# Two token blocks read as rows and transposed on TensorE, K and Q weights stored by head, W2 at other addresses

## The reference

```python
xn = rmsnorm(x, norm_mix_g)
u = xn @ w_in                       # 5120 columns: b, c, v (512 each) | q, k, v (512 each) | 2 x 1024 gates
y_a = (b_g * causal_conv3(c_g * v_a)) @ w_a_out
o = diff_attention(q, k, v, lam, alibi_slopes)   # 4 heads, two softmax maps of width 64, values of 128
y_b = (rmsnorm(o, subln_g) * (1 - lam_init)) @ w_b_out
x = x + (sigmoid(gate_a) * y_a + sigmoid(gate_b) * y_b) @ w_o
h = rmsnorm(x, norm_mlp_g) @ w_mlp_in            # 4096 columns
x = x + square(relu(h)) @ w_mlp_out
return rmsnorm(x, norm_final_g)
```

## Time and profile before

| | |
|---|---|
| time, median of 3 runs (lowest to highest) | 1285.27 us (1283.91 to 1289.87) |
| the profiled execution, its own time | 1275.98 us |
| its span, slowest core (core 4) | 1274.5 us |
| spans of all cores | 1249.3 to 1274.5 us |
| TensorE busy, instructions | 1155.0 us (91%), 7066 |
| ScalarE, VectorE, GpSimd busy | 541.4 us (42%), 472.9 us (37%), 90.9 us (7%) |
| chain that ended last, by engine | PE 75%, DMA 8%, ACT 4%, DVE 4%, issue 4% |
| of it, by line | L404 (all matmuls) 75%, DMA of W2 4%, ACT L677 4%, DMA of xs 2%, DMA of wc 2% |
| TensorE waiting for the loads of W2 (core 4) | 28.9 us in 15 waits |

### The profile page before, as it was taken

How to read it: one execution, slowest core, us unless ns; L and a number is a source line. 1 busy time by engine, 2 the same in 40 slices (tenths; PEclk the granted TensorE clock), 3 DMA queues, 4 the chain that set the end, 5 groups by cost and what they waited for, 6 DMA issues and landing times.

```text
span 1274.5 us, 20401 instructions; the slowest of 8 cores (1249.3 to 1274.5 us)
## 1 busy us (share of the span) xinstructions
PE 1155.0 (91%) x7066; PEld 553.3 (43%) x7066; DVE 472.9 (37%) x1079; ACT 541.4 (42%) x740; POOL 90.9 (7%) x148
## 2 busy tenths in 40 slices
PE   6887788998999999999999999937999999999996
PEld 3343444444444454454444444412444444444442
DVE  2437367465345534324445534200222222122211
ACT  0385665586556787777623223300033013103300
POOL 3212101010001001000000002000000000000000
PEclk9989899998999999999999999966999999999998
DMA  9965723230216437375294708940130003012001
GB/s 155 244 180 100 149 84 72 74 79 10 38 44 128 95 63 151 53 173 135 37 233 116 231 1 184 194 112 6 67 99 1 33 33 99 2 58 75 1 34 50
DMA packets 67412, 117.75 MB, mean 92 GB/s; under 512 B 37072, under 2 KB 39376, under 8 KB 66288
## 3 DMA queue, kind: packets, MB, share of 16 engines
q0 software_dynamic: 14544, 44.11, 20.5%
q1 hardware_dynamic: 52768, 72.34, 19.4%
HBM read 120.69 MB, written 29.36 MB: 118 GB/s over the span
## 4 chain that ended last, share of the span: by engine, by line
PE 75%; DMA 8%; ACT 4%; DVE 4%; issue 4%; another core or an unknown queue 2%; POOL 1%; DVEq 0%; ACTq 0%; SPq 0%; POOLq 0%
PE ps_all L404 75%; DMA big<-w 4%; ACT big L677 4%; DMA big<-xs 2%; DMA big<-wc 2%; POOL big L409 1%; ACT big L448 1%; DVE big L624 0%; DMA xm_sp<-big 0%; DVE big L615 0%; DVE big L617 0%; DMA big<-xT 0%; DVE big L819 0%; DVE big L558 0%
## 5 line engine op out<-in xcount | busy, mean ns | idle before, releaser
L404 PE MATMUL ps_all<-big 128*128 128x512 bf16 (+7 forms) x7066 | 1155.0, 329 | 107.0 <-DMA big<-w 28.9
L404 PEld LDWEIGHTS ps_all<-big 128*128 128x128 bf16 (+2 forms) x7066 | 553.3, 99 | 708.2 <-issue 266.7
L677 ACT ACTIVATE big<-ps_all,big 128x1024 bf16<-128x1024 f32 (+3 forms) x384 | 337.6, 926 | 122.9 <-PE ps_all L404 110.0
L920 ACT ACTIVATE big<-ps_all 128x512 bf16<-128x512 f32 x128 | 76.3, 597 | 140.8 <-PE ps_all L404 140.5
L937 ACT ACTIVATE big<-big 128x1024 bf16<-128x1024 f32 x16 | 16.9, 1056 | 247.3 <-DVE big L932 247.3
L921 DVE TENSOR_TENSOR big<-big 128x512 bf16<-128x512 bf16 x128 | 54.5, 425 | 159.9 <-ACT big L920 159.5
L932 DVE SCALAR_TENSOR_TENSOR big<-ps_all,big 128x512 f32<-128x512 f32 x32 | 24.0, 751 | 199.1 <-PE ps_all L404 199.1
L819 DVE SCALAR_TENSOR_TENSOR big<-big,ps_all 128x512 f32<-128x512 f32 x64 | 43.8, 687 | 115.1 <-PE ps_all L404 114.7
L808 ACT ACTIVATE big<-ps_all,big 128x512 f32<-128x512 f32 x64 | 43.6, 686 | 81.4 <-PE ps_all L404 81.4
L448 ACT ACTIVATE big<-big 128x1024 bf16<-128x1024 f32 x32 | 33.8, 1057 | 39.1 <-DMA big<-xs 38.3
L939 POOL TENSOR_TENSOR big<-big 128x1 f32<-128x1 f32 x16 | 8.7, 545 | 461.7 <-DVE big L938 461.7
(11 more groups left out here) (67 smaller groups left out, 301.1 us busy)
## 6 DMA issues: line engine op xcount, KB each, us to landing
big<-xs SPq DMA_DIRECT2D x40, 512.0 KB, 5.3
big<-w POOLq DMA_DIRECT2D x32, 512.0 KB, 12.5
xm_sp<-big SPq DMA_DIRECT2D x16, 512.0 KB, 4.3
big<-xm_sp SPq DMA_DIRECT2D x16, 512.0 KB, 4.9
out<-big SPq DMA_DIRECT2D x16, 512.0 KB, 2.6
big<-xT POOLq DMA_DIRECT2D x24, 256.0 KB, 5.8
big<-xs POOLq DMA_DIRECT2D x8, 512.0 KB, 18.5
xn_sp<-big SPq DMA_DIRECT2D x4, 1024.0 KB, 4.5
```

The lines of the kernel that those rows point to most:

```text
L404: S.op("pe", lambda e: e.matmul(out, lhsT, rhs, start=start, stop=stop, skip_group_check=skip), reads, writes)
L677: act(lambda e, a=a, b=b, c=c, s=s, PT=PT, scale=scale: e.activation(PT.ap[:, :, a:b], Sb[s][:, :, a:b], AF.Exp, bias=ccol(C_BTAB + c), sc ...
L920: act(lambda e: e.activation(r.ap, ps, AF.Relu), [key], [r])
```

## The change

At the start, the transposed blocks 4 and 0 are no longer loaded. The order on GpSimd's queue is Wv, the 4 token tiles of block 4, Wk and Wq in four loads each (now one buffer per head, 128 x 8 x 128), and XT of block 5. `from_tokens` takes a token tile: a cast to bf16 on VectorE, the Square on ScalarE, eight transposes on TensorE into one PSUM bank, one copy by ScalarE into all 8 buffers of XT (128 columns of each), and the reciprocal rms of this tile alone. `values` runs it one tile ahead of `v_chunk`. V of block 4 comes first, then K of block 4, each head with `fold_head`, a multiplication of 128 x 1024 with the gain broadcast; then V of block 0, whose token tiles are loaded from SP's queue; the halo loads and block 5's tiles follow there. The list W now begins with K of block 0 and the fold of Wq, and then Q.

In the MLP, the tiles of W2 get other addresses: 0 and 1 over the attention's buffers, 28 to 31 over the two late g_x buffers, 2 to 13 over Wg2 to Wg5 and g_xn, 14 to 21 over Wo, 22 to 27 over g_xb, g_t and g_m. The load of 0 and 1 is issued 12 steps after the attention, the six of 2 to 13 in the last gate stage behind the emission of the first tile's output projection, and the remaining nine where all 16 stood.

```diff
-    Wk = [ar.take("Wk%d" % c, [512], BF16) for c in range(8)]
+    Wk = [ar.take("Wk%d" % h, [8, 128], BF16) for h in range(4)]
     Wv = [ar.take("Wv%d" % c, [512], BF16) for c in range(8)]
-    Wq = [ar.take("Wq%d" % c, [512], BF16) for c in range(8)]
+    Wq = [ar.take("Wq%d" % h, [8, 128], BF16) for h in range(4)]
...
+    tok_bf = Ring([area(c_hb.lo, c_ac.hi).take("tok_bf0", [1024], BF16),
+                   area(c_hb.lo + 2 * K1, c_ac.hi).take("tok_bf1", [1024], BF16)])
...
-    W2 = [am.take("W2_%d" % f, [1024], BF16) for f in range(6)]
+    w2_end = [am.take("W2_%d" % f, [1024], BF16) for f in (28, 29, 30, 31)]
+    W2 = [am.take("W2_%d" % f, [1024], BF16) for f in range(2)]
...
-    w2_hi = [am.take("W2_%d" % (18 + f), [1024], BF16) for f in range(8)]
-    W2 += [am.take("W2_%d" % (6 + f), [1024], BF16) for f in range(12)]
+    w2_hi = [am.take("W2_%d" % (14 + f), [1024], BF16) for f in range(8)]
+    W2 += [am.take("W2_%d" % (2 + f), [1024], BF16) for f in range(12)]
     W2 += w2_hi
...
-    W2 += [am.take("W2_%d" % (26 + f), [1024], BF16) for f in range(6)]
+    W2 += [am.take("W2_%d" % (22 + f), [1024], BF16) for f in range(6)] + w2_end
...
+    def fold_head(w):
+        dve(lambda e: e.tensor_tensor(w.ap, w.ap, ccol(C_GMIX, 8).unsqueeze(2).to_broadcast([128, 8, 128]), ALU.mult),
+            [w, cst], [w])
...
-                mm(ps, Wk[c].ap[:, h * 128:(h + 1) * 128], x[c].ap, c == 0, c == 7, [Wk[c], x[c]], [key])
+                mm(ps, Wk[h].ap[:, c, :], x[c].ap, c == 0, c == 7, [Wk[h], x[c]], [key])
...
-    for q in range(4):
-        wload(Wk, wk_d, 2 * q, 2, 512)
-        wload(XT[0], xT_d[4], 2 * q, 2, 512)
     slot_of[4], slot_of[0], slot_of[5] = 0, 1, 2
     for q in range(2):
         wload(Wv, wv_d, 4 * q, 4, 512)
-    for q in range(2):
-        wload(XT[1], xT_d[0], 4 * q, 4, 512)
     for t in range(4):
         tok_pool(4, t)
+    for h in range(4):
+        wload(Wk, wk_d, h, 1, 1024)
+    for h in range(4):
+        wload(Wq, wq_d, h, 1, 1024)
     for q in range(2):
-        wload(Wq, wq_d, 4 * q, 4, 512)
+        wload(XT[2], xT_d[5], 4 * q, 4, 512)
     consts()
-    halo_load()
...
-    warm(40)
-    ps4 = [obank() for h in range(4)]
-    for c in range(8):
-        fold_gain(Wk, c)
-        for h in range(4):
-            mm(ps4[h][0], Wk[c].ap[:, h * 128:(h + 1) * 128], XT[0][c].ap, c == 0, c == 7, [Wk[c], XT[0][c]],
-               [ps4[h][1]])
-    for h in range(4):
-        k_evac(4, h, *ps4[h])
-    warm(16)
+    def from_tokens(blk, t):
+        x, s, n = tok[(blk, t)], slot_of[blk], slice(t, t + 1)
+        xb = tok_bf.next()
+        dve(lambda e: e.tensor_copy(xb.ap, x.ap), [x], [xb])
+        stat_tile(blk, t, x)
+        ps, key = obank()
+        pb = ps.bitcast(BF16).rearrange("p (c t) -> p c t", c=8)
+        for c in range(8):
+            S.op("pe", lambda e, c=c: e.transpose(pb[:, c, :], xb.ap[:, c * 128:(c + 1) * 128], ident),
+                 [xb, cbf], [key])
+        dst = span(XT[s]).rearrange("p (c t) -> p c t", c=8)[:, :, t * 128:(t + 1) * 128]
+        act(lambda e: e.copy(dst, pb), [key], XT[s])
+        a, b, k = ss1[blk].ap[:, n], rs1[blk].ap[:, n], ksc[blk].ap[:, n]
+        dve(lambda e: e.tensor_scalar(a, a, 1.0 / D, EPS, ALU.mult, ALU.add), [ss1[blk]], [ss1[blk]])
+        S.op("pool", lambda e: e.tensor_tensor(b, a, m05.ap[:, n], ALU.pow), [ss1[blk], m05], [rs1[blk]])
+        dve(lambda e: e.tensor_scalar_mul(k, b, 0.125), [rs1[blk]], [ksc[blk]])
+
+    def values(blk):
+        from_tokens(blk, 0)
+        for t in range(4):
+            if t + 1 < 4:
+                from_tokens(blk, t + 1)
+            v_chunk(blk, t)()
+
+    warm(24)
     for c in range(8):
         fold_gain(Wv, c)
-    for f in stats(4, None):
-        f()
+    values(4)
     for t in range(4):
-        tok_pool(0, t)
-    for q in range(2):
-        wload(XT[2], xT_d[5], 4 * q, 4, 512)
+        tok_load(0, t)
+    for h in range(4):
+        fold_head(Wk[h])
+        k_chunk(4, h)()
+    values(0)
+    halo_load()
+    for h in range(4):
+        tok_load(5, h)
...
-    W += [(1, f) for f in vs(4)]
-    W += [(1, f) for f in ks(0)] + [(0, lambda: [fold_gain(Wq, c) for c in range(8)])]
-    W += [(0, f) for f in stats(0, 5)] + [(1, f) for f in vs(0)]
+    W += [(1, f) for f in ks(0)] + [(0, lambda: [fold_head(w) for w in Wq])]
...
-    W += G_list(3, None)
+    g3 = G_list(3, None)
+    k = max(n for n, (w, f) in enumerate(g3) if w == 1) - 7
+    for n in range(6):
+        g3.insert(k + n, (0, lambda n=n: w2_load(2 + 2 * n, 2)))
+    W += g3
...
+    deferred.append((12, lambda: w2_load(0, 2)))
     deferred.append((24, lambda: m_load(0)))
...
-    w2_load(0, 18)
-    w2_load(18, 8)
-    w2_load(26, 6)
+    w2_load(14, 18)
     m_load(1)
```

More of the change, by code:

```diff
@@ L566, in q_mm @@
         for c in range(8):
-            mm(ps, Wq[c].ap[:, h * 128:(h + 1) * 128], x[c].ap, c == 0, c == 7, [Wq[c], x[c]], [key])
+            mm(ps, Wq[h].ap[:, c, :], x[c].ap, c == 0, c == 7, [Wq[h], x[c]], [key])
         return ps, key
@@ L1202, in make_in_maps @@
     flat = lambda a: np.ascontiguousarray(a).reshape(128, -1)
+    heads = lambda a: flat(a.reshape(128, 8, 4, 128).transpose(0, 2, 1, 3))
     w = rows(inputs["w_in"][0])
@@ L1211, in make_in_maps @@
     common = {
-        "wk": flat(w[:, :, 2048:2560]), "wv": flat(w[:, :, 2560:3072]), "wq": flat(w[:, :, 1536:2048]),
+        "wk": heads(w[:, :, 2048:2560]), "wv": flat(w[:, :, 2560:3072]), "wq": heads(w[:, :, 1536:2048]),
         "wc": flat(wc), "wg": flat(wg), "wa": flat(rows(inputs["w_a_out"][0])),
```

## The result

The changed kernel takes **1298.8 us** (median; 1296.4 to 1300.5), the kernel before, run beside it, 1284.6: a ratio of 1.011 with an interval of 1.0065 to 1.015. It is slower by about 1.1%. Times and ratios here are of the fast executions; those with a lower clock on one die, or over 1.5% above the fastest of their kernel, are left out. The profiled execution took 1298.1 us.

The account below looks back on a forecast made before the run. TensorE, busy 91% of the span, bounds the kernel; time changes only in its waits at the start and first MLP block. Core 4: 1274.5 + 38 - 39 + 12 = 1285.5, with span 1287, plus 3 offset: 1290; range 1268 to 1310.

Parts of the forecast that it names:

- the side held likeliest: Outcome against the kernel before: slower 0.47, same (1279 to 1292) 0.27, faster 0.26.
- the sum: Whole kernel, core 4: 1274.5 + 38 - 39 + 12 = 1285.5; core 0: 1279.5; with span and offset 1290.
- The start, +38 on core 4: Start up to the first QK matmul: serial tile chain +27.7 at full clock, plus 10.6 for the clock.
- The clock's price: TensorE's lowered clock at the start, 49% busy: between +0 and +26.5 us, taken at 40%, +10.6.
- Rival (1): Start at 1.2 GHz throughout: +54 instead of +38, 1306 us; chance 0.24.
- 1.1 us more per tile for slow transposes: Start: transposes at 1.8 us a tile, 1.1 more on each of six tiles on the chain, giving 1297.
- On core 4 I keep a remainder: First MLP block, core 4: four W2 pairs still come after the transposing load; 12 us lost, bounds 0 and 19.
- Rival (2): Start stays at 2.4 GHz and W2 arrives in time on every core; 1274 us with offset; chance 0.28.
- rival (3): W2 loads don't help die 1, transposing load holds its engine until 834: remainder 19 and more, 1297 to 1310; chance 0.08.
- the last sentence: Last output projection: the prediction is wrong if six W2 loads under it delay its x tiles; no size given.
- The Trainium skill's turn-taking: W2 wait: DMA engines alternate between queues packet by packet, so pairs would keep half the engine, remainder 0; not adopted.
- The offset: Profiled run to median: shown runs' median 9.3 longer, put down to the W2 wait; a third left, 3 us carried.

Follow-up runs that it names:

- w2_only: The W2 half of the change alone on the kernel before, with the start of before: 1259.7 us, ratio 0.981.
- before_tr_late: The kernel before with one wait more: block 1's transposing load issued behind the landing of the last W2 tiles; 1251.3 us, ratio 0.977.
- w2_x_early: The kernel before with the W2 half and x tiles 2 and 3 of the last output projection loaded early: 1254.5 to 1270.8 us, ratio 0.982.
- w2_x_tr_late: The kernel before with the W2 half, early x tiles and block 1's transposing load behind the last W2 tiles: 1244.9 us, ratio 0.9705.
- start_only: The changed start alone on the kernel before, W2 loads issued where they were before: 1309.6 us, ratio 1.018.
- start_order: The whole change with its start reordered: block 4's tiles transposed before any V matmul, folds ahead of heads; 1273.3 us, ratio 0.9945.
- start_fill: The whole change with idle matmuls of 256 columns in TensorE's waits at the start: 1287.5 us, ratio 1.006.
- after_tr_late: The whole change with block 1's transposing load behind the last W2 tiles, x tiles loaded where the change has them: 1297.1 us, ratio 1.012.

## Why the prediction held, and where its steps did not

The measured 1298.8 lies 9 above the predicted 1290, inside the range and on the side held likeliest. But that is luck in part: the sum took core 4 for the slowest, where it is core 5, and two of its steps were wrong in opposite senses.

- **The start, +38 on core 4: right, in size and in make-up.** Measured + 38.2. At full clock the steps gave a first QK at 89.1; with the waits filled it is 88.65. Transposes 0.61 (0.72 taken, with the drain), ScalarE's copy 1.01 (1.1), fold 1.22 (1.2), V tiles 5.35 apart with the clock held (5.3), K heads 3.96 (3.84). The clock's price, taken at 10.6 as a value between two bounds, is 10.9; that it came so near is luck. That order and not loads or engines sets the pace was shown by the reordering.
- **Where the low clock falls: taken as a mean, in truth by phase.** On core 4 the V matmuls of the first three tiles of each block were granted 0.50 to 0.56, those of the fourth and the transposes between them 1.00, the K heads 1.00 until the last. Rival (1), 1.2 GHz throughout, fell with the K heads; its 1.1 us more per tile for slow transposes fell with the 0.61. The Trainium skill (TensorE: Matmul & The Clock Gate, Part 4, PE-mode transpose) gives about 275 ns for one transpose, by which an estimate is 2.2 us for eight; the rows give 0.61 for eight in a run at 2.4 GHz and 1.01 at 1.2, so the measurement decides against the figure for such a run of eight. That the time by that figure, 1299, is the measured one is chance; what the page says of a transpose's busy time was not tested by itself.
- **"On core 4 I keep a remainder", 12 us: wrong, it is 0.** TensorE waits for W2 on no core. The step reckoned with a transposing load that starts beside the loads and holds the pairs until it ends. In the rows of before it held them for 8 us (109 GB/s), and when the pairs came one by one, the DMA engines stood nearly idle (0.07, in the earlier trace rows too). In the changed kernel the six early loads are issued 27 us or more ahead of it (on core 4 the last four at 799.83, it at 826.69), and it took 18.8 us there. Rival (2) had this half right, and rival (3) fell with it.
- **The x tiles: the step that was missing.** The sum had no term for what the six early loads do to SP's loads behind them; only the last sentence named it. It cost 14.6 to 18.6 us on one core of each pair. The steps for core 4, with the remainder at 0, give 1273.5, and core 4 measured 1273.3. The run with the x tiles early and the transposing load late shows what is left without the x wait: 1282.0 as the median, all cores from 1272.7 to 1278.9.
- **The cause of the W2 wait before: seen, but not followed up.** The prediction put the late pairs down to the transposing load and yet costed the change by when the loads are issued. Earlier issues do remove the wait (w2_only), but before_tr_late shows that they aren't needed for most of it: one wait on SP, with W2 issued as late as before, takes 39.0 on core 4 down to 5.6.
- **The Trainium skill's turn-taking** (DMA: Bandwidth & Descriptors, queues, rings and completion order) was read as: beside the transpose the pairs keep half the engine, remainder 0. On core 4 of the kernel before the trace is in line with turns by packet: from 796 to 828 GpSimd's queue had 1580 packets (5.74 MB, 179 GB/s) and SP's 1671 (0.43 MB), so the W2 loads lost little then. On core 0 of w2_x_early it does not: 63 against 917 packets from 804 to 820, and 29 GB/s in all. The remainder of 0 in the changed kernel came by the early issues, not by turns.
- **The offset.** 3 us were carried from the profiled execution to the median; the profiled execution of the changed kernel is 0.7 below its median. The spread of before may be the transposing load's: the runs of w2_x_tr_late lie within 2 us of each other, those of before beside them from 1271 to 1287; but of the four of before_tr_late, with that one edit, one lies 10 us above the others.

Open: why the W2 wait was smaller with the later start (start_only), why the transposing load takes 88 us on one core and 24 on another (w2_x_early, cores 0 and 1; on core 1 its packets ran from 806 to 812.4, when GpSimd's queue had 80 packets beside 4189 of SP's), why only one core of a pair waits for x, and the last 2.8 us of core 5's sum.

## What to carry to other kernels

When loads land late, look first at what else moves on the same DMA engines in that stretch and at the GB/s, before moving the loads themselves: here one transposing load held back behind the last load gave as much (ratio 0.977) as new addresses and early issues together (0.981). A DMA share near one engine's part while loads are awaited is a sign of its own: the rate of all is then not what is short. Here loads that were issued early delayed what was due sooner on the other queue; list what the other queue has to deliver in that window, and put that ahead. In a start that runs tile by tile through four engines, emit the feeding steps of all tiles before the first consumer, since a buffer that is tracked as a whole turned every tile here into a serial chain, and the waits cost the clock as well.

## What the runs showed of the hardware

- A transposing load of 1 MiB lands in 6 to 8 us with the DMA engines to itself (before_tr_late, w2_x_tr_late) and in 24 to 88 us in w2_x_early, where it is issued among the converting loads of W2. At worst the core's whole traffic falls to 33 GB/s with all engines busy (core 0); on core 4 of the kernel before it stays at 190.
- Where the x wait appears, it is always on the core of a pair that reaches the last output projection later by its own count from its first instruction: 20 pairs of 20, in five kernels (the changed one, w2_only, start_order, start_fill, after_tr_late). On core 4 the same x tiles, issued as long behind the same W2 loads, were in by 823, 12 us after the issue; on core 5 they took up to 29. While W2 loads run alone on both (before_tr_late, 808 to 832 us), cores 4 and 5 write 170 and 171 GB/s; as these loads read f32 and write bf16, they read twice that, some 341 each. The Trainium skill (HBM Reference, Specifications) says that the two cores of a domain share its bandwidth and get about 358 GB/s each; the rate agrees, but that the sharing makes the later core wait was not tested by itself.
- On core 4 of the changed kernel the granted clock was 0.50 in the V matmuls from 20.4 to 24.1, 1.00 in the transposes behind a wait at 25.6 and 0.53 in the next V matmuls, and it held at 1.00 in the first three K heads, with waits of 1.3 to 2.1 us in both phases.
